# A fused two-block transformer kernel: the filler matmuls behind the embedding go, its last output is copied one row earlier, and four modulation columns change places in the weight stream

## What is computed

```
mod = silu(c) @ w_ada + b_ada                    # 9 vectors of 1024, i.e. 72 columns of 128
# first block
u = rmsnorm(x) * (1 + mod[0,1]) + mod[0,0]
h = x + 0.5 * mod[0,2] * swiglu(u, w_gu (1024 x 5632), w_down (2816 x 1024))
u = rmsnorm(h) * (1 + mod[1,1]) + mod[1,0]
h = h + mod[1,2] * mixer(u)                      # q, k, v, short convolution, stick-breaking attention, gates
u = rmsnorm(h) * (1 + mod[2,1]) + mod[2,0]
h = h + 0.5 * mod[2,2] * swiglu(u, ...)
h = rmsnorm(h)
# second block
x = h + gated(gmlp, forgetting attention);  x = x + convglu(x)
x = x + (p @ w_ple) * sigmoid(rmsnorm(x) @ w_ple_gate)     # "the embedding" is p @ w_ple
out = rmsnorm(x)
```

## Time and profile before

| | |
|---|---|
| median of three runs | 2083.33 us (2082.55 to 2088.31) |
| profiled execution, time | 2082.47 us |
| profiled execution, span from first to last instruction | 2080.7 us |
| PE busy | 2048.1 us, 98% of the span |
| DVE, ACT, POOL busy | 52%, 39%, 4% |
| mean granted clock of PE | 0.993 of 2.4 GHz |
| shares of the chain that ended last | PE 93%, DVE 3%, issue 2%, ACT 1%, POOL 1% |

### The profile page before, as it was taken

How to read it: one execution, slowest core, us unless ns; L and a number is a source line. 1 busy time by engine, 2 the same in 40 slices (tenths; PEclk the granted TensorE clock), 3 DMA queues, 4 the chain that set the end, 5 groups by cost and what they waited for, 6 DMA issues and landing times.

```text
span 2080.7 us, 25297 instructions
## 1 busy us (share of the span) xinstructions
PE 2048.1 (98%) x10327; PEld 1719.4 (83%) x10327; DVE 1090.1 (52%) x1682; ACT 810.0 (39%) x1265; POOL 92.4 (4%) x128
## 2 busy tenths in 40 slices
PE   7999999989999999999999999999999999999997
PEld 6888888878888898888888887778888888888887
DVE  7444444577854554333335645765425475446546
ACT  6322232345544333222224435565323354234334
POOL 1000000100000010000002000000000100000012
PEclk8999999999999999999999999999999999999999
DMA  8544533443432223223222332222332222332241
GB/s 350 199 137 158 182 101 128 146 171 113 142 112 92 92 71 122 73 100 113 84 84 87 122 113 81 71 77 97 101 92 96 77 102 83 107 105 95 70 150 41
DMA packets 71062, 235.76 MB, mean 113 GB/s; under 512 B 8850, under 2 KB 11154, under 8 KB 70563
## 3 DMA queue, kind: packets, MB, share of 16 engines
q1 hardware_dynamic: 68768, 226.07, 32.5%
q0 software_dynamic: 2032, 7.90, 1.2%
q10 hardware_dynamic: 146, 0.18, 0.0%
HBM read 229.37 MB, written 4.75 MB: 113 GB/s over the span
## 4 chain that ended last, share of the span: by engine, by line
PE 93%; DVE 3%; issue 2%; ACT 1%; POOL 1%; DMA 0%; DVEq 0%; POOLq 0%; ACTq 0%
PE bank L719 82%; PE bank L783 4%; PE bank L1146 1%; PE bank L1132 1%; PE bank L1028 1%; PE bank L900 1%; PE bank L903 1%; DVE w_lo L1720 1%; PE bank L926 1%; DMA w_raw<-in_w_mix_dram 0%; POOL ssq L2340 0%; PE bank L1058 0%; PE bank L814 0%; DVE w_raw L1716 0%; PE bank L1178 0%
## 5 line engine op out<-in xcount | busy, mean ns | idle before, releaser
L1720 DVE TENSOR_TENSOR w_lo<-w_raw,w_hi 128x1024 fp32r<-128x1024 f32 (+2 forms) x343 | 392.7, 1171 | 196.9 <-ACT w_hi L1243 196.5
L719 PE MATMUL bank<-u_hi,w_hi 128*128 128x512 f32 (+1 forms) x1904 | 491.5, 371 | 0.0
L719 PE MATMUL bank<-u_lo,w_hi 128*128 128x512 f32 (+1 forms) x1904 | 489.5, 369 | 1.2 <-DVE u_lo L1763 1.2
L719 PE MATMUL bank<-u_hi,w_lo 128*128 128x512 f32 (+1 forms) x1904 | 490.4, 369 | 0.0
L1243 ACT ACTIVATE w_hi<-w_raw 128x1024 fp32r<-128x1024 f32 (+2 forms) x343 | 324.4, 977 | 227.8 <-PE bank L719 171.2
L719 PEld LDWEIGHTS bank<-u_lo,w_hi 128*128 128x128 f32 x1904 | 353.8, 189 | 60.2 <-DVE u_lo L1763 1.6
L719 PEld LDWEIGHTS bank<-u_hi,w_hi 128*128 128x128 f32 x1904 | 354.3, 189 | 58.6 <-issue 0.7
L719 PEld LDWEIGHTS bank<-u_hi,w_lo 128*128 128x128 f32 x1904 | 353.3, 189 | 57.5
L1848 DVE TENSOR_TENSOR ff_a<-ff_s,bank 128x512 f32<-128x512 f32 x44 | 30.2, 687 | 242.1 <-issue 210.6
L1319 ACT ACTIVATE act_hi<-ff_a 128x512 fp32r<-128x512 f32 x66 | 41.7, 632 | 262.4 <-DVE ff_a L1848 222.3
L719 PE MATMUL bank<-act_hi,w_lo 128*128 128x512 f32 (+1 forms) x561 | 130.1, 377 | 0.0
(11 more groups left out here) (292 smaller groups left out, 2189.1 us busy)
## 6 DMA issues: line engine op xcount, KB each, us to landing
w_raw<-in_w_gu_dram SPq DMA_DIRECT2D x112, 512.0 KB, 4.0
w_raw<-in_w_ada_dram SPq DMA_DIRECT2D x49, 512.0 KB, 4.5
w_raw<-in_w_mix_dram SPq DMA_DIRECT2D x36, 512.0 KB, 3.6
w_raw<-in_w_dn_dram SPq DMA_DIRECT2D x44, 384.0 KB, 3.1
w_raw<-in_w_dn_dram SPq DMA_DIRECT2D x44, 320.0 KB, 3.3
w_raw<-in_w_in_dram SPq DMA_DIRECT2D x24, 512.0 KB, 4.0
w_raw<-in_w_o_dram SPq DMA_DIRECT2D x16, 512.0 KB, 3.5
w_raw<-in_w_in_g_dram SPq DMA_DIRECT2D x16, 512.0 KB, 3.5
```

The lines of the kernel that those rows point to most:

```text
L719: m = e.matmul(bank[b][:, c], w, (x.lo if part == 2 else x.hi)[:, k, c], start=start, stop=stop, skip_group_check=True)
L1720: e.tensor_tensor(lo_of(name), raw_of(i), f32(hi_of(name)), ALU.subtract).then_inc(*s_w_lo.inc(name))
```

## The change

Three edits. (1) `FIRST_STEPS` loses both groups of fillers, 8 behind `embed(7)` and 6 before pair 2, and the step (1, 0) now stands before (0, 1). (2) On ACT the copy of `embed(7)` moves from behind `first_high(3)` to before `first_high(2)`. (3) The stream no longer has an "a" behind each of mv0 to mv3; instead the pairs 8, 10, 12 and 14 of the first feed-forward net have two behind them in place of one. All columns after that stand earlier by up to four, in the same order; from tile m8 on the stream is what it was.

```
-FIRST_STEPS = ((0, 0), ("embed", 7), ("warm", 8), (0, 1), (1, 0), (1, 1), ("warm", 6), (2, 0), (2, 1),
+FIRST_STEPS = ((0, 0), ("embed", 7), (1, 0), (0, 1), (1, 1), (2, 0), (2, 1),
                *[(g, k) for k in range(2, 8) for g in range(3)])
...
                     weight(f"{tag}u{m}", io[w_gu][NFF + m])
-                    between()
+                    for _ in range(2 if m in (8, 10, 12, 14) else 1):
+                        between()
...
     for k in range(4):
         weight(f"mv{k}", io["w_mix_v"][k])
-        some_ada()
...
-            if g == "warm":
-                warm(i, 7)
-            elif g == "embed":
+            if g == "embed":
                 embed(i)
...
         embed(6)
+        embed(7)
         first_high(2)
         first_high(3)
-        embed(7)
         first_high(4)
```

12 lines of the change are left out of this document (5 added, 7 removed).

## The result

The changed kernel takes 2061.98 us (median of 4 runs, 2061.65 to 2063.03), the kernel before 2082.94 us beside it (4 runs, 2082.22 to 2088.31). The ratio is 0.9895, with a 95% interval from 0.9878 to 0.9912: about 21 us faster. The forecast was 2060, with 2055 to 2068 as the range. The profiled execution of the changed kernel is the slowest of its four, 2063.03 us with a span of 2061.3 us; against the span of before, 2080.7 us, that is 19.4 us less. The sum of the prediction was 23.4 us.

The account below looks back on a forecast made before the run. PE, busy for 98% of the span, was taken as the bound. Gains of 15.4 + 1.2 + 6.8 = 23.4 us off 2082.47 gave 2059.1, and 0.9 more for the median 2060 us; range 2055 to 2068.

Parts of the forecast that it names:

- Term 1: At the start: idle time, fillers and slower matmuls go, less 1.9 us of new short waits; 15.4 us gained.
- the lower bound: At the start: all eight steps of rows 0 to 2 run at the lower clock, leaving a gain of 6.1 us.
- Term 2: Boundary before the mixer: PE's wait for u_lo of the second half's row 3 goes; 1.2 us, between 0 and 1.3.
- term 3: At the values: PE's 5.1 us wait for ScalarE's copy of v_a and 1.7 us of lower clock go; 6.8 us.
- the text's worse case: At the values: transfers take 4.6 us as in the crowded stretch, and 0.6 us of PE's wait come back.
- rival C: The values stay late through a slipping transfer or VectorE's keys; PE waits 1 to 5 us, 2061 to 2067; chance 0.13.
- Columns in the net: Four more columns in pairs 8 to 14 cost nothing under VectorE's idle 4.98 us; without that cover 5.1 us.
- B: At the start: without fillers the clock falls after short gaps, losing 1.7 to 9.3 us; 2062 to 2069, chance 0.14.
- D: First feed-forward net: late loads of pairs 5 and 6 give back up to 15.4 us; 2064 to 2075, chance 0.04.
- E: At the start: without fillers the clock doesn't come back once PE has work with gaps; up to 2091 us, chance 0.02.
- the clock's place in each execution: Whole kernel: the allowance around the forecast of 2060, giving 2056 to 2063 us.
- a gain beyond 26 us: Start at its upper bound of 17.3 us, or better transfers elsewhere; chance 0.04.

Follow-up runs that it names:

- after: The changed kernel with all three edits, against the kernel before: 2061.98 us, ratio 0.9895.
- start only: Kernel before with fillers gone, step (1, 0) ahead of (0, 1) and the copy of embed(7) early, stream unchanged: 2071.71 us, ratio 0.9943.
- fillers only: Kernel before with only the 14 fillers taken out; step order, late copy of embed(7) and stream stay: 2069.66 us, ratio 0.9936.
- stream alone: Kernel before with only the four columns moved behind pairs 8 to 14; fillers and start stay: 2076.89 us, ratio 0.9971.

## Why the prediction was right

**Term 1, 15.4 us: right.** 15.2 measured in three kernels with very different other edits (after, start only, fillers only). Its steps hold: row 3 begins at 43.20 as computed (43.2), and VectorE's split of pair 2 and its u_lo of row 3 are what is late next. The 1.9 us of new short waits came out too: 12.03, 3.79 and 1.34 us went, 15.2 were gained, so 2.0 us came back, though only 0.6 of them are recorded as idle time. The choice against the lower bound (6.1 us, all eight steps at the lower clock) was the important one, and the granted clock of 1.00 over 30 to 63 us bears it out. What the prediction left unsaid is where the gain sits: taking out the fillers gives all of it, the early copy by itself 8.4 us, the first group of fillers by itself 5.8 us, and the two together no more than the fillers alone.

**Term 2, 1.2 us, and term 3, 6.8 us: 6.2 measured instead of 8.0.** PE begins the first group of scores at 440.14, where before it did at 456.77; less the start's 15.2 that is 1.4 us for term 2:

```profile
440.14 0.33 PE L899 MATMUL bank<-qs,ks 128*128 128x384 f32 x1
```

The rest, 4.8 us by V, is term 3. (PE's recorded wait for u_lo in the boundary, 1.15 us, is gone in the stream alone as well, and stays in the start alone.) Of the wait of 5.08 us, 1.86 us stayed, and the low clock behind it went as forecast (1.00 in 442.7 to 446.4 us, where before had 0.54), with 1.6 of its 1.7 us. The step that was mis-sized is one: m18's way from issue to landing. The issues came when the prediction had them (m4 at 427.54, m0 at 429.81, m14 at 433.48 us, all within 0.3 us of 443.0, 445.2 and 448.6 less 15.4), and PE wanted bank 6 at 440.83. But m18 took 5.76 us and not 3.4, nor the 4.6 of the text's worse case. The price of 3.4 us had been read from m8 before, in a stretch in which the DMA share was 0.63, against 0.95 for m18 now:

```profile
444.20:447.60 3.40, 3.40 (x17) 2.81 (x16) 3.40 (x4) 0.01 (x1) 0.00 (x0) 1.00 0.63 200
```

The trace before held the right price, 5.67 us for m18 itself in the same place of the stream. With it the prediction's own sum would have been: issued at 434.4, landed at 440.1, split at 441.1, copied by 442.2, against bank 6 wanted at 440.7: an estimate of 1.5 us of wait left, where 1.86 came. That case was rival C, at its mild end. With three more columns out of the way both terms together give 8.3 us (342.79 - 334.48), a little more than the 8.0 of the forecast.

**Columns in the net: nothing, right,** for four and for seven of them; fourteen more, from pair 4 on, cost 1.1 us, and there by a late transfer, which the prediction's reasoning (VectorE's idle time covers them) had not priced.

**The other rivals.** B (the fillers keep the clock up) falls for the start: with the fillers out the clock stays at 1.00 over 30 to 63 us through gaps of 0.2 to 0.8 us. That holds for this stretch and not everywhere: near 1110 us it falls in seven profiles with no idle time recorded but 0.69 us ahead of it. The page that spoke for B, the Trainium skill's TensorE: Matmul & The Clock Gate, section "A second HAM failure mode: psum-queue depth-cycling", describes a clock that swings where PE idles briefly between groups of matmuls; this trace does not agree with it for the start, where no swing shows. D falls: PE has no wait at 60 to 120 us. E falls with B.

**What the sum left out.** 2.0 us of low clock in two places that the change doesn't touch. The prediction had allowed for this only as "the clock's place in each execution". 23.4 less 0.2, 1.8 and 2.0 is the 19.4 of the spans. The profiled execution of after was its slowest, 1.05 us above the median, where the forecast had put the median 0.9 us above. So 2060 was off by 2 us, from errors of 4 us in the sum and 2 the other way between one execution and the median; that the two partly cancel is luck. The chances of the outcomes (0.94 faster, 0.03 and 0.03) also leave out the 0.04 that had been given to a gain beyond 26 us, which is faster too.

## What to carry to other kernels

Ask of a filler first what it waits for: here its bank, not its matmuls, was the price, and ScalarE's late copy of that bank cost nothing once nobody asked for it. When you shorten one wait in a chain of transfers, price each transfer by its own row in the trace before, not by a neighbour's: m8's 3.4 us stood for m18, whose own row said 5.67. And before an instruction is pulled ahead of a split on an engine, look at which engine needs that split: the copy that removed a wait of 1.2 to 1.9 us brought 0.8 us back, because VectorE then got the tile's high part late, and the softplus behind it waited. And when you compare stretches of two traces, count from the engine that the stretch hangs on: counted from PE's matmuls the same start differs by 0.6 us, counted from VectorE's split by 0.01.
